# One block, one core: experts chosen per row tile, first expert's rows gathered turned, residual put back by ScalarE

## The reference

```python
def moe_ffn(hn, w_router, b_router, w_gate_up, b_gate_up, w_down, b_down):
    ...
    logits = (tok @ w_router + b_router).astype(jnp.float32)
    top_v, top_i = lax.top_k(logits, TOP_K)
    top_w = jax.nn.softmax(top_v, axis=-1)
    dense_w = jnp.sum(jax.nn.one_hot(top_i, N_EXPERTS, dtype=jnp.float32) * top_w[..., None], axis=1).astype(tok.dtype)
    out = jnp.zeros_like(tok)
    for e in range(N_EXPERTS):
        gu = tok @ w_gate_up[e] + b_gate_up[e]
        gate, up = gu[:, :EXPERT_FF], gu[:, EXPERT_FF:]
        gate = jnp.minimum(gate, SWIGLU_LIMIT)
        up = jnp.clip(up, -SWIGLU_LIMIT, SWIGLU_LIMIT)
        act = (up + 1.0) * (gate * jax.nn.sigmoid(SWIGLU_ALPHA * gate))
        out = out + dense_w[:, e:e + 1] * (act @ w_down[e] + b_down[e])
    ...
        h = h + hybrid_mixer(...)
        h = h + moe_ffn(rms_norm(h, norm2_g[layer]), w_router[layer], ...)
    h = rms_norm(h, final_g)
```

## Time and profile before

| | |
|---|---|
| median of 3 runs | 1419.91 us (1418.66, 1419.91, 1420.15) |
| profiled execution | 1418.49 us, span 1416.7 us |
| PE busy | 97% of the span, 6501 matmuls |
| DVE, ACT, POOL busy | 27%, 16%, 4% |
| DMA | 475.23 MB, 335 GB/s over the span |
| mean granted PE clock | 0.989 |

### The profile page before, as it was taken

One profiled execution on the slowest core, in us unless ns is written; L12 is line 12 of the kernel. 1 busy time (PEld: TensorE's weight loads), 2 busy tenths in 40 slices (PEclk: granted clock), 3 DMA queues, 4 the chain that ended last, 5 costly groups with the idle time before them and its releaser, 6 DMA issues.

```text
span 1416.7 us, 15675 instructions
## 1 busy us (share of the span) xinstructions
PE 1369.5 (97%) x6501; PEld 677.9 (48%) x6501; DVE 377.6 (27%) x822; ACT 230.1 (16%) x491; POOL 50.4 (4%) x33
## 2 busy tenths in 40 slices
PE   9999999999999999999999999999999999999997
PEld 7888845887788533333333333333333333333332
DVE  6666846363101131211111111111111111111211
ACT  2226622143200120100001000010011000100111
POOL 0503210000000000000000000000000000000000
PEclk9999999999999999999999999999999999999999
DMA  9465233431348499999999999999999999999996
GB/s 368 182 217 189 109 149 119 156 142 60 120 178 360 164 378 421 432 433 431 433 431 430 429 432 433 435 429 431 430 427 421 431 417 413 410 431 430 430 428 257
DMA packets 26172, 475.23 MB, mean 335 GB/s; under 512 B 4272, under 2 KB 4432, under 8 KB 7152
## 3 DMA queue, kind: packets, MB, share of 16 engines
q1 hardware_dynamic: 26080, 474.56, 80.1%
q10 hardware_dynamic: 48, 0.03, 0.0%
HBM read 473.50 MB, written 1.08 MB: 335 GB/s over the span
## 4 chain that ended last, share of the span: by engine, by line
PE 62%; DMA 32%; DVE 3%; ACT 2%; issue 1%; SPq 0%; POOL 0%; DVEq 0%; POOLq 0%; ACTq 0%
DMA weights<-in_w_gate_up_dram 31%; PE ps L1019 22%; PE ps L591 6%; PE ps L1045 5%; PE ps L723 4%; PE ps L798 4%; PE ps L788 4%; PE ps L712 2%; PE ps L884 2%; PE ps L898 2%; PE ps L555 2%; PE ps L1055 1%; PE ps L978 1%; PE ps L617 1%; ACT weights L1120 1%
## 5 line engine op out<-in xcount | busy, mean ns | idle before, releaser
L1019 PE MATMUL ps<-weights,hnT 128*64 128x512 f32 x1992 | 451.2, 608 | 29.0 <-DMA weights<-in_w_gate_up_dram 29.0
L1019 PEld LDWEIGHTS ps<-weights,hnT 128*64 128x64 f32 x1992 | 144.2, 140 | 320.5 <-issue 267.3
L1045 PE MATMUL ps<-weights,ssmT 128*64 128x512 f32 x1008 | 223.4, 595 | 0.7 <-ACT ssmT L1123 0.7
L1123 ACT ACTIVATE arena<-ps 128x512 f32<-128x512 f32 (+5 forms) x115 | 48.1, 443 | 661.7 <-PE ps L555 550.9
L1736 DVE TENSOR_SCALAR ssmT<-ps 128x512 f32<-128x512 f32 x32 | 22.1, 691 | 471.7 <-PE ps L1019 471.7
L1045 PEld LDWEIGHTS ps<-weights,ssmT 128*64 128x64 f32 x1008 | 69.5, 137 | 131.8 <-issue 125.6
L591 PE MATMUL ps<-hnT,weights 128*128 128x272 f32 (+1 forms) x352 | 80.8, 391 | 0.0
L1123 ACT ACTIVATE hnT<-ps 128x512 f32<-128x512 f32 x63 | 37.7, 598 | 254.6 <-PE ps L1045 223.1
L591 PEld LDWEIGHTS ps<-hnT,weights 128*128 128x128 f32 x352 | 66.7, 190 | 13.2 <-issue 0.2
L1055 PE MATMUL ps<-hnT,arena 64*128 64x512 f32 x256 | 63.6, 615 | 0.8 <-DVE hnT L1771 0.8
L1716 DVE TENSOR_SCALAR ssmT<-const,arena 128x64 f32<-128x64 f32 x64 | 13.3, 251 | 190.4 <-PE ps L995 190.3
(11 more groups left out here) (235 smaller groups left out, 1015.5 us busy)
## 6 DMA issues: line engine op xcount, KB each, us to landing
weights<-in_w_gate_up_dram SPq DMA_DIRECT2D x52, 4096.0 KB, 20.2
weights<-in_w_down_dram SPq DMA_DIRECT2D x27, 4096.0 KB, 17.4
weights<-in_w_blocks_dram SPq DMA_DIRECT2D x28, 2048.0 KB, 8.9
weights<-in_w_gate_up_dram SPq DMA_DIRECT2D x7, 3072.0 KB, 17.4
weights<-in_w_gate_up_dram SPq DMA_DIRECT2D x8, 2048.0 KB, 10.2
weights<-in_w_down_dram SPq DMA_DIRECT2D x4, 2048.0 KB, 15.4
arena<-in_w_gate_up_dram SPq DMA_DIRECT2D x6, 1024.0 KB, 12.5
weights<-in_w_down_dram SPq DMA_DIRECT2D x2, 3072.0 KB, 17.0
```

The costliest lines, as they stand in the source:

```text
L1019: mm = pe.matmul(bank(4 + b)[64 * a:64 * a + 64, :], xe[:, 2 * (k % 4) + k // 4, :], w[:, FF * b + 512 * a:FF * b + 512 * a + 512], start= ...
L1045: mm = pe.matmul(bank(7)[64 * c:64 * c + 64, :], actT[:, P * j + SLOTS * a:P * j + SLOTS * a + SLOTS], pair[kk % 2][:, 512 * c:512 * c + 5 ...
L1123: return nc.scalar.activation(o, i, ACT.Copy)
```

## The change

- The norm's root and factor are made per row tile (`squares_sum(t)`, `rooted2(t)`, `rstd(t)`), and ACT's normed rows `hn2` (`normed`) come in three pieces: tile 0 in halves, tile 1 whole.
- `choose(t)` works on one row tile: logits, `max`, the last four of the eight greatest overwritten with a constant by `memset`, `match_replace` writes that constant over the four greatest logits, and a comparison with the constant is `routed`. The two tiles' logits lie in one bank.
- `ranks(t)` and `places(t)` do the same per tile.
- `gather_first` computes the first expert's rows already turned: `hn2`'s 128-column blocks are the weights and `sel` (64 columns) the moving side, 16 matmuls into banks 7 and 6, and DVE's `first_tokens(a)` multiplies each half by the gains. The copy by ACT and the transposes are gone for unit 0, and unit 0's gate-up starts on `first_xe`, the first half.
- Unit 0's bias matmuls and `turn_weights` (now with the counts of rows per expert, 32 x 32) stand between the tiles 3 and 4 of its gate-up.
- The residual is put back into banks 0 to 3 by ACT copies (`reopen`, semaphore `opened`), not by `open_sum` on PE. The SP queue waits for `opened` 4 and `hn2_ok` 3 before the load into `hrow`; later counts of `scat_ps` are one lower.
- The softmax weights come from the exponentials of all 32 logits times `routed`, not of the four greatest.
- `rstd1` and `mask_ok` are replaced by the chain semaphore of DVE.

```diff
             sp.wait_ge(logit_ps, 2)
             load_held(held_gu[5:6])
-            sp.wait_ge(hn2_ok, RT)
-            sp.wait_ge(scat_ps, 1)
+            sp.wait_ge(hn2_ok, 3)
+            sp.wait_ge(opened, 4)
             load_held(held_gu[6:])
             for first, last in FIRST_TILES:
                 sp.wait_ge(gu_free, last)
...
-            def open_sum(t, c):
-                return pe.matmul(bank(2 * t + c), ident, hrow[:, t, 512 * c:512 * c + 512], start=True, stop=False, skip_group_check=True)
+            def ranks(t):
+
+                pe.wait_ge(routed_ok, t + 1)
+                mm = pe.matmul(bank(5)[:, 32 * t:32 * t + 32], tri_lt, routed[:, t, :], start=(t == 0), stop=True, skip_group_check=True)
+                if t == 0:
+                    mm = pe.matmul(bank(5)[:, 32:64], ones, routed[:, 0, :], start=False, stop=False, skip_group_check=True)
+                mm.then_inc(rank_ps, 1)
+
+            def gather_first(t, ks):
+
+                pe.wait_ge(hn2_ok, t + 2)
+                pe.wait_ge(sel_ok, t + 1)
+                for k in ks:
+                    mm = pe.matmul(bank(7 - k // 4)[:, SLOTS * (k % 4):SLOTS * (k % 4) + SLOTS], hn2[:, t, P * k:P * k + P], sel[:, t, :],
+                                   start=(t == 0 and k % 4 == 0), stop=(t == 1), skip_group_check=True)
+                    if t and k % 4 == 3:
+                        mm.then_inc(first_ps, 1)
...
             out_proj(1, 1, range(4, KD))
             router(1, 0)
             turn_rows(1, (1,))
-            open_sum(0, 0)
+            ranks(0)
             router(1, 1)
-            open_sum(0, 1)
-            open_sum(1, 0)
-            open_sum(1, 1).then_inc(scat_ps, 1)
-
-            pe.wait_ge(routed_ok, 1)
-            pe.matmul(bank(7)[:, 0:64], tri_lt, routed.rearrange("p t e -> p (t e)"), start=True, stop=True)
-            pe.matmul(bank(7)[:, 32:64], ones, routed[:, 0, :], start=False, stop=True, skip_group_check=True).then_inc(route_ps, 1)
+            gather_first(0, range(5))
+            ranks(1)
+            gather_first(0, range(5, KD))
+            gather_first(1, range(KD))
...
-                    mm = turn(bank(7)[0:EXPERTS, P * t:P * t + P], dense_w[:, t, :])
-                mm.then_inc(route_ps, 1)
+                    turn(bank(7)[0:EXPERTS, P * t:P * t + P], dense_w[:, t, :])
+                for t in range(RT):
+                    mm = pe.matmul(bank(7)[0:EXPERTS, 2 * P:2 * P + EXPERTS], ones[:, 0:EXPERTS], routed[:, t, :], start=(t == 0), stop=(t == RT - 1))
+                mm.then_inc(weights_ps, 1)
...
+            def unit(u, ahead, peeled=False, first=False, owed=True, biases=()):
+
+                if first:
+                    pe.wait_ge(first_xe, 1)
+                    gate_up(u, peeled, range(4), start=True)
+                    pe.wait_ge(bias_part, 6)
+                    bias(u, start=False)
+                    turn_weights()
+                    gate_up(u, peeled, range(4, KD))
+                else:
+                    gate_up(u, peeled)
...
-            gather(0)
-            pe.wait_ge(bias_part, 6)
-            pe.matmul(bank(4)[:, 0:EXPERTS], ones, routed[:, 0, :], start=True, stop=False)
-            pe.matmul(bank(4)[:, 0:EXPERTS], ones, routed[:, 1, :], start=False, stop=True).then_inc(route_ps, 1)
-            turn_tokens(0, into=6)
-            pe.wait_ge(count_ok, 1)
-            start_bias(0, first=True)
-            turn_weights()
-            pe.wait_ge(xe_ok, 1)
-            unit(0, True, owed=False)
+                    bias(u + 1)
+
+            unit(0, True, first=True, owed=False)
+            pe.wait_ge(opened, 4)
...
+                act_f(hn2[:, t, cols_of], hrow[:, t, cols_of], ACT.Copy, scale=rstat[:, 6 + t:7 + t]).then_inc(hn2_ok, 1)
+
+            def reopen(t, c):
+
+                copy(bank(2 * t + c), hrow[:, t, 512 * c:512 * c + 512]).then_inc(opened, 1)
...
             square(0, 1)
+            rooted2(0)
             rows_turned(0)
             square(1, 0)
+            for t, c in ((0, 0), (0, 1), (1, 0)):
+                reopen(t, c)
+            act_e.wait_ge(wo_ps, 4)
+            normed(0, slice(0, 512))
             square(1, 1)
             rows_turned(1)
-            act_e.wait_ge(rstd2, 1)
-            act_f(rstat[:, 6:8], rstat[:, 6:8], ACT.Sqrt, scale=1.0 / D, bias=stat[:, 8:9]).then_inc(rstd2, 1)
+            rooted2(1)
+            normed(0, slice(512, D))
+            normed(1)
+            reopen(1, 1)
             act_f(stat[:, 11:12], stat[:, 8:9], ACT.Exp)
-            act_e.wait_ge(rstd2, 3)
-            act_f(hn2[:, 0, :], hrow[:, 0, :], ACT.Copy, scale=rstat[:, 6:7]).then_inc(hn2_ok, 1)
-            act_f(hn2[:, 1, :], hrow[:, 1, :], ACT.Copy, scale=rstat[:, 7:8]).then_inc(hn2_ok, 1)
-            act_e.wait_ge(negv_ok, 1)
             for t in range(RT):
-                i = act_f(e4[:, t, 0:4], v8[:, t, 0:4], ACT.Exp, bias=rstat[:, 8 + t:9 + t], accum_out=rstat[:, 10 + t:11 + t])
-            i.then_inc(e4_ok, 1)
+                act_e.wait_ge(logit_ok, 3 + t)
+                act_f(exped[:, t, :], logit[:, t, :], ACT.Exp, bias=rstat[:, 8 + t:9 + t]).then_inc(exped_ok, 1)
...
+            def choose(t):
+
+                dve.wait_ge(rstd2, 3 * t + 3)
+                dve.wait_ge(logit_ps, t + 1)
+                V.scalar_tensor_tensor(out=logit[:, t, :], in0=bank(4)[:, 64 * t:64 * t + EXPERTS], scalar=rstat[:, 6 + t:7 + t],
+                                       in1=br_bc, op0=ALU.mult, op1=ALU.add).then_inc(logit_ok, 1)
+                dve.wait_ge(logit_ok, t + 1)
+                link(V.max(v8[:, t, :], logit[:, t, :]))
+                link(V.memset(v8[:, t, TOP_K:8], PICKED))
+                link(V.match_replace(marked[:, t, :], v8[:, t, :], logit[:, t, :], PICKED))
+                V.tensor_scalar(routed[:, t, :], marked[:, t, :], PICKED, None, ALU.is_equal).then_inc(routed_ok, 1)
+
+            def places(t):
+                dve.wait_ge(routed_ok, t + 1)
+                dve.wait_ge(rank_ps, t + 1)
+                link(V.scalar_tensor_tensor(out=posm[:, t, :], in0=bank(5)[:, 32 * t:32 * t + 32], scalar=UNROUTED, in1=routed[:, t, :],
+                                            op0=ALU.add, op1=ALU.mult))
+                V.tensor_scalar(sel[:, t, :], slots[:, 0, 0:SLOTS], posm[:, t, 0:1], None, ALU.is_equal).then_inc(sel_ok, 1)
...
+            squares_sum(0)
             rows_turned(0)
+            rstd(0)
             rows_turned(1)
+            choose(0)
+            V.tensor_scalar(one_expert[0:96, :], cst("row_expert")[0:96, :].broadcast_to([96, SLOTS]),
+                            cst("experts")[0:96, 0:1], None, ALU.is_equal).then_inc(hot_ok, 1)
             residual(1, 1)
-            dve.wait_ge(sq2, 4)
-            V.tensor_tensor(rstat[:, 6:8], rstat[:, 0:4:2], rstat[:, 1:4:2], ALU.add).then_inc(rstd2, 1)
...
-            V.tensor_reduce(routed, pick.rearrange("p t (i e) -> p t e i", i=TOP_K), AX.X, ALU.add).then_inc(routed_ok, 1)
-            V.tensor_scalar(rstat[:, 8:10], v8[:, :, 0:1].rearrange("p a b -> p (a b)"), -1.0, None, ALU.mult).then_inc(negv_ok, 1)
-            dve.wait_ge(routed_ok, 1)
-            dve.wait_ge(route_ps, 1)
-            link(V.scalar_tensor_tensor(out=posm, in0=split(bank(7)[:, 0:64], 2), scalar=UNROUTED, in1=routed, op0=ALU.add, op1=ALU.mult))
+            squares_sum(1)
+            places(0)
+            rstd(1)
+            choose(1)
+            V.tensor_scalar(rstat[:, 8:10], v8[:, :, 0:1].rearrange("p a b -> p (a b)"), -1.0, None, ALU.mult).then_inc(logit_ok, 2)
+            places(1)
...
+            def first_tokens(a):
+                dve.wait_ge(first_ps, a + 1)
+                V.tensor_tensor(xe_flat.rearrange("p (j a s) -> p j a s", j=4, a=2)[:, :, a, :], split(bank(7 - a)[:, 0:4 * SLOTS], 4),
+                                g2_cols[:, 4 * a:4 * a + 4].unsqueeze(2).broadcast_to([P, 4, SLOTS]),
+                                ALU.mult).then_inc(xe_ok if a else first_xe, 1)
...
-            select(0, 0, None)
-            dve.wait_ge(e4_ok, 1)
+            first_tokens(0)
+            first_tokens(1)
+            dve.wait_ge(exped_ok, 2)
+            link(V.tensor_tensor(exped, exped, routed, ALU.mult))
+            link(V.tensor_reduce(rstat[:, 10:12], exped, AX.X, ALU.add))
             link(V.reciprocal(rstat[:, 10:12], rstat[:, 10:12]))
-            link(V.tensor_tensor(w4[:, :, 0:4], e4[:, :, 0:4], rstat[:, 10:12].unsqueeze(2).broadcast_to([P, 2, 4]), ALU.mult))
-            link(V.tensor_tensor(pick4, pick4, w4[:, :, 0:TOP_K].unsqueeze(3).broadcast_to([P, 2, TOP_K, EXPERTS]), ALU.mult))
-            V.tensor_reduce(dense_w, pick.rearrange("p t (i e) -> p t e i", i=TOP_K), AX.X, ALU.add).then_inc(dense_ok, 1)
-            dve.wait_ge(route_ps, 2)
-            V.tensor_copy(count[0:1, :], bank(4)[0:1, 0:32]).then_inc(count_ok, 1)
-            tokens_in(0, of=6)
```

129 lines of the change are left out of this document (58 added, 71 removed).

## The result

| | before | after |
|---|---|---|
| median of 20 runs each | 1419.17 us (1415.76 to 1420.58) | 1422.76 us (1418.60 to 1424.59) |
| after / before | | 1.0022, 95% interval 1.0015 to 1.0030 |
| profiled execution | 1418.49, span 1416.7 | 1418.83, span 1417.0 |
| mean granted PE clock | 0.989 | 0.988 in the profiled run, 0.985 to 0.988 in all |

The changed kernel is slower by about 3 us. Its profiled execution is one of its fastest, so this one execution by itself would have shown no change. In a second comparison the pair came out at 1.0041 (1.0028 to 1.0055).

What follows compares the result with a forecast made beforehand. The stream of weights was taken to set the pace. Closing its 3.2 us hole takes 1418.49 to 1415.3, or 1417.0 with a slow stretch behind the last wait; median forecast 1416.4, range 1414.5 to 1418.8.

Steps and rivals of the forecast that it cites:

- rival B: At the bridge: PE runs the start of gate-up at the lower clock, 1.7 us lost, end 1417.6; chance 0.14.
- Choice on one tile: DVE's choice for router tile 1 at the bridge: 1.1 us in sum, ready at 497.4, 1.4 earlier.
- `opened` and the load into `hrow`: ACT's last reopening copy near 497.7, then SP's early load at 497.8, 1.1 earlier than 498.91.
- First expert matmul at 500.0: PE at the start of expert 0's gate-up: 500.0 instead of 504.49, a lead of 4.5 us.
- Inserts in gate-up: Bias matmuls, weight transposes and count matmuls inside expert 0's gate-up: together 1.0 us of at most 1.4.
- Lead behind them 3.5: PE's lead behind the inserts in unit 0: 3.5 us (2.9 to 4.0), kept through units 0 and 1.
- Load of expert 1's first tile at 502.0: SP queue: issue at 502.0 instead of 506.47, while two early loads still move, so the hole closes.
- The hole worth 3.2: DMA engines running dry around 504 to 512: closing that gap in the weights' stream gains 3.2 us.
- The estimate from the Trainium skill: Size of the same DMA hole by the skill's fixed transfer times: hole and gain 2.7 us.
- The smaller of the two leads counts: At unit 2's first load (537.29): PE's lead of 3.5 just suffices, so the smaller number, 3.2, counts.
- D: Unit 0: lower clock for the whole first gate-up; at 7 us lost the end is 3.5 later, 1423; chance 0.06.
- The end: Behind the last wait, 1362.06: PE's clock level makes 1.7 us by chance, so 1415.3 or 1417.0, median 1416.4.

Runs made afterwards that it cites:

- second comparison: The unedited changed kernel timed again beside the kernel before: 1423.42 against 1417.95 us, ratio 1.0041.
- wide gathers: Changed kernel with each of the 16 turned gathers streaming its 64 columns twice (128 moving columns): 1417.03 us, ratio 0.9997; second profiled execution 1417.10.
- all three wide: Changed kernel with router, ranks and turned gathers at 128 moving columns: 1416.59 us, ratio 0.9987.
- wide router: Changed kernel with router and ranks alone at 128 moving columns, gathers still 64 wide: 1416.96 us, ratio 0.9989.
- PE pushed: Changed kernel with router and ranks at 128 columns, plus four 512-column matmuls of constants ahead of the first expert matmul: 1418.78 us, ratio 1.0005.
- before with ScalarE's copies and the wide router: Kernel before with ScalarE copies putting the residual back instead of PE's opening matmuls, router and ranks at 128 moving columns: 1421.51 us, ratio 1.0029.
- the three other kernels with its order of PE: Kernel before with ScalarE copies for PE's opening matmuls (1.0029); that with router and ranks at 128 columns (1.0029); that with four 512-column constant matmuls (1.0006).

## Why the prediction was wrong

The step that failed is rival B's weighing. I let the clock stay at the upper level because before, too, PE had done small work and had waited 0.94 without a fall. That row was read without what stood in front of it: the four 512-wide opening matmuls, which the change took out. Put back (1.0010), replaced by constants (the kernel before: 1.0006 for 1.0029), or made needless by wider columns (0.9987 to 0.9997), the clock stays. At the wait near 1136 the fall makes PE 4.2 us later, as the account below shows; I had let it cost nothing in the forecast and 1.7 us in rival B.

By the steps of the prediction:

- Choice on one tile, 1.1 us, `routed` at 497.4: right (497.41). Memset 0.06, replacement with its load 0.26, compare 0.18 lie within their bounds. `opened` and the load into `hrow`: right, 0.35 early.
- First expert matmul at 500.0, lead 4.5: at full clock it is 500.69, lead 3.8. I counted the four gathers up to `first_xe`; PE's list has all eight of tile 1 ahead of gate-up. With the clock it is 502.51 (503.10 and 503.60 in the second and fifth execution).
- Inserts in gate-up 1.0: 1.1 (507.61 to 508.71), right. Lead behind them 3.5: it is 2.75 at full clock (511.46 less 508.71), -0.1 in the first execution of after (511.55) and -1.5 in the fifth (512.98).
- Load of expert 1's first tile at 502.0: 502.67 at full clock, 505.51 in after.
- The hole worth 3.2: about right. Four profiled executions (wide gathers twice, all three wide, wide router) have the clock at 1.00 and the hole closed. In them expert 1's last piece lands at 536.6 to 537.6, mean 537.1, against 540.0 in the two of before. PE's wait near 1136 ends at 1133.09 on average, against 1136.10, so 3.0 earlier. The wait at unit 4 shows only 1.8 of that (616.15, 616.36, 616.51 and 615.50, mean 616.13, against 617.95). A single 4 MB piece between them takes 10.3 to 11.0 us for the usual 9.7, in ten of the eleven profiled executions with the changed order of PE, at either clock, and none takes over 10.1 in the five with the order of before. By 1136 this is made up again; its cause is open. The estimate from the Trainium skill, 2.7 us (DMA: Bandwidth & Descriptors, sections Anatomy of one DMA, and Latency and other measured facts), and my 3.2 lie on either side of 3.0.
- The smaller of the two leads counts: right. With wide columns the second half of unit 0 starts 2.6 earlier than in before and the wait near 1136 ends 3.0 earlier; in after it starts 0.7 later and that wait ends 1.2 later. The place I gave for it is not borne out. The stream was to stand still at unit 2, behind expert 1's last piece. The next piece lands 9.7 us behind that one in the first execution of before and with PE pushed, and 9.8 to 10.1 in four of the five of after (11.0 in the third), so a standstill there would be 0.4 us at most in these four. PE's lateness is in the stream already within expert 1. The first hole stays open, and the 2 MB piece that PE releases behind the inserts lands 5.9 us after the piece ahead of it (519.1 to 525.1), against 4.9 in before (519.6 to 524.5) and with wide gathers.
- Rival B priced the fall at 1.7. It was 2.0 on the gathers and 1.0 to 1.8 on gate-up's first half. The cause is B's, the way to the end is D's, with a smaller loss: D reckoned with 7 us lost, and 2.8 (first execution) to 4.3 (fifth) were enough to eat the 2.75 that PE really had. B and D together had a chance of 0.20 and stood apart as if they were two things; they are one, at two sizes. The Trainium skill's rule that a transpose doesn't count as busy the way a matmul does (TensorE: Matmul & The Clock Gate, section Part 4: PE-mode transpose) spoke for B. No run here tests its rule by itself: the same transposes stand in the bridge of the kernels whose clock stayed at 1.00.
- The end: I gave the fall of the clock behind the wait near 1361 (1.7 us) as a matter of chance, and that is borne out. A second such term, the last output transfers, I didn't have; it is in the table below.

**The account.** PE's position can be followed through the whole run. Means over the profiled executions, with the four with wider columns of the list above:

| | before (2) | after (5) | wider columns (4) |
|---|---|---|---|
| second half of unit 0 starts | 511.39 | 512.08 | 508.77 |
| wait at unit 4 ends | 617.95 | 619.75 | 616.13 |
| wait near 1136 ends | 1136.10 | 1137.26 | 1133.09 |
| wait near 1361 ends (unit 30) | 1361.09 | 1362.35 | 1358.00 |
| from there to the end of the span | 54.6 | 56.6 | 57.6 |
| clock falls behind it | 0 of 2 | 3 of 5 | 4 of 4 |
| output transfers hold SP for over 2.6 us | 0 of 2 | 3 of 5 | 3 of 4 |
| span | 1415.7 | 1418.9 | 1415.6 |

At 1136 after is 1.2 later than before, where 3.2 earlier was forecast. Of these 4.4 us the low clock is 4.2 (1137.26 less 1133.09, shown by the kernels with wider columns) and the size of the hole 0.2. The rest of after's loss is behind 1361, and it has two terms. From that wait to the end of the span are 54.6 us where the clock doesn't fall and the last three output transfers hold the SP queue for 1.85 us (three executions). With the fall alone they are 56.2 to 56.3 (seven executions), with the longer output transfers alone 56.6 (one), and with both 57.7 to 58.4 (five). Both terms stand in the lines of unit 30 and of the output in the wide gather, to be read against 7.09 in the earlier trace rows and against before's output:

```profile
1358.90 8.68 PE L1031 MATMUL ps<-weights,hnT 128*64 128x512 f32 x32 [2.25 <-DMA weights<-in_w_gate_up_dram]
...
1410.66 2.90 SPq L510 DMA_DIRECT2D out_dram<-arena  x3
```

```profile
1412.22 1.85 SPq L512 DMA_DIRECT2D out_dram<-arena  x3
```

This is also why the kernels with wider columns, 3 us ahead at 1361, end only 0.1% or less ahead of before: the end took 3 us longer in the executions that I profiled.

The late falls, near 1137 and near 1361, are no likelier where the clock fell at the bridge. A fall behind the wait near 1137 makes the way to the wait near 1303 longer by 1.4 (1137.27 to 1304.64, 167.4, in the second execution; 1136.47 to 1302.43, 166.0, in the first). Where the clock fell at the bridge, the seven profiled executions have 8 of the 14 possible late falls; the nine others have 11 of 18. That before has none near 1361 in its two may be chance, since the three other kernels with its order of PE all have it. The longer output transfers stand in six of the eleven executions with the changed order of PE, three of them with the clock at 1.00 in the bridge, and in none of the five with the order of before. What makes them longer is open. So is how often either term falls in the executions without a profile: after's five took 1420.79 on average, and the median of its twenty is 2.0 higher.

The wait at unit 4 alone would mislead here. The kernel pushed at full clock has it at 619.50 and is at 1.0005, while before with ScalarE's copies and the wide router has it at 619.59 and is at 1.0029. By the wait near 1361 they are 2.7 apart (1360.73 and 1363.47). That the fall costs time is shown by the pairs above; how much of the median's 3.6 us (5.5 in the second comparison) is the bridge's is known only for the profiled executions, 1.2 to 1.3 us of a mean difference of 3.2.
